# First up projection as seven half-size products per pair (Strassen's scheme), with the channel stage in six parts

## What is computed

```python
D_MODEL, SEQ, CTX_LEN = 1024, 512, 256
D_FF = ((8 * D_MODEL // 3 + 127) // 128) * 128      # 2816, 22 tiles of 128

def conv_ffn(h, w_up, conv_w, conv_b, w_down):
    u = h @ w_up                                    # tokens x 1024 by 1024 x 5632
    u = depthwise_conv_width_3(u, conv_w) + conv_b  # along the tokens
    g, v = jnp.split(u, 2, axis=-1)
    return (jax.nn.silu(g) * v) @ w_down

x_lat = x_lat + g2x * conv_ffn(modulate(rmsnorm(x_lat, g_ffn), sh2x, sc2x), ...)
x_ctx = x_ctx + g2c * conv_ffn(modulate(rmsnorm(x_ctx, g_ffn), sh2c, sc2c), ...)
```

## Time and profile before

| | |
|---|---|
| median of 3 runs | 1761.22 us (1761.12 to 1761.82) |
| profiled execution: time, span | 1760.48 us, 1758.7 us |
| mean granted TensorE clock | 0.979 |
| TensorE busy | 1658.7 us, 94% |
| VectorE, ScalarE, GpSimd busy | 1120.0, 769.9, 617.5 us |
| first layer's channel stage, about | 480 to 1034 us |

### The profile page before, as it was taken

One profiled execution on the slowest core, in us unless ns is written; L12 is line 12 of the kernel. 1 busy time (PEld: TensorE's weight loads), 2 busy tenths in 40 slices (PEclk: granted clock), 3 DMA queues, 4 the chain that ended last, 5 costly groups with the idle time before them and its releaser, 6 DMA issues.

```text
span 1758.7 us, 25943 instructions
## 1 busy us (share of the span) xinstructions
PE 1658.7 (94%) x9530; PEld 1403.9 (80%) x9530; DVE 1120.0 (64%) x1749; ACT 769.9 (44%) x1273; POOL 617.5 (35%) x311
## 2 busy tenths in 40 slices
PE   5999998889799999999999998999888999999997
PEld 3778786778688888888888886888666888888887
DVE  7986677677876575767245774677664864254256
ACT  6546676463253311332123344666554543243242
POOL 0356560210123243323422307564222154444442
PEclk9899999999899999999999999999999999999999
DMA  9520000024222333433434423000012133233232
GB/s 393 178 93 25 25 25 13 25 109 150 90 96 87 116 121 108 134 117 120 144 120 131 144 96 96 25 25 25 25 37 96 48 120 97 94 95 106 87 99 91
DMA packets 45533, 168.24 MB, mean 96 GB/s; under 512 B 4736, under 2 KB 6784, under 8 KB 43520
## 3 DMA queue, kind: packets, MB, share of 16 engines
q1 hardware_dynamic: 40896, 156.50, 26.4%
q10 hardware_dynamic: 4544, 10.49, 1.6%
HBM read 161.73 MB, written 5.24 MB: 95 GB/s over the span
## 4 chain that ended last, share of the span: by engine, by line
PE 73%; DVE 7%; issue 3%; ACT 2%; POOL 1%; DMA 1%; DVEq 0%; ACTq 0%; SPq 0%; POOLq 0%
PE ps L1254 22%; PE ps L1255 21%; PE ps L1256 21%; PE ps L1385 3%; PE ps L1399 2%; DVE junk_mid L2150 1%; PE ps L1418 1%; DVE sqsum L2220 1%; DVE nb L2408 1%; PE ps L1419 1%; DVE p_sb L2426 1%; POOL w_lo L1136 1%; ACT ptmp L1919 1%; DMA w_raw<-w_d 1%; DVE ht L2247 0%
## 5 line engine op out<-in xcount | busy, mean ns | idle before, releaser
L1136 POOL TENSOR_TENSOR w_lo<-w_raw,w_hi 128x1024 fp32r<-128x1024 f32 x175 | 444.3, 2541 | 933.2 <-ACT w_hi L1700 893.9
L1254 PE MATMUL ps<-h_hi,w_hi 128*128 128x512 f32 (+1 forms) x1592 | 570.3, 358 | 14.5 <-DVE h_lo L2255 6.8
L1255 PE MATMUL ps<-h_lo,w_hi 128*128 128x512 f32 (+1 forms) x1592 | 558.8, 351 | 0.0
L1256 PE MATMUL ps<-h_hi,w_lo 128*128 128x512 f32 (+1 forms) x1592 | 558.4, 351 | 0.0
L1254 PEld LDWEIGHTS ps<-h_hi,w_hi 128*128 128x128 f32 x1592 | 304.6, 191 | 63.4 <-issue 24.7
L1256 PEld LDWEIGHTS ps<-h_hi,w_lo 128*128 128x128 f32 x1592 | 304.2, 191 | 39.9
L1255 PEld LDWEIGHTS ps<-h_lo,w_hi 128*128 128x128 f32 x1592 | 305.1, 192 | 35.5
L1700 ACT ACTIVATE w_hi<-w_raw 128x1024 fp32r<-128x1024 f32 x188 | 198.3, 1056 | 240.8 <-PE ps L1256 222.5
L1254 PE MATMUL ps<-a_hi,w_hi 128*128 128x512 f32 (+1 forms) x552 | 191.8, 347 | 1.2 <-DVE a_lo L2622 1.2
L1255 PE MATMUL ps<-a_lo,w_hi 128*128 128x512 f32 (+1 forms) x552 | 191.5, 347 | 0.0
L1256 PE MATMUL ps<-a_hi,w_lo 128*128 128x512 f32 (+1 forms) x552 | 191.1, 346 | 0.0
(11 more groups left out here) (186 smaller groups left out, 2414.1 us busy)
## 6 DMA issues: line engine op xcount, KB each, us to landing
w_raw<-w_d SPq DMA_DIRECT2D x188, 512.0 KB, 3.5
ada_b<-ada_d SPq DMA_DIRECT2D x56, 512.0 KB, 4.2
ada_first<-first_d SPq DMA_DIRECT2D x8, 1024.0 KB, 20.4
ada_lead<-ada_d SPq DMA_DIRECT2D x14, 512.0 KB, 3.6
ada_mid<-ada_d SPq DMA_DIRECT2D x10, 512.0 KB, 5.1
x_sb<-x_d SPq DMA_DIRECT2D x2, 1536.0 KB, 9.0
x_sb<-x_d ACTq DMA_DIRECT2D x1, 3072.0 KB, 11.9
x_spill_d<-x_sb ACTq DMA_DIRECT2D x1, 2048.0 KB, 7.8
```

What stands on the lines that cost most here:

```text
L1136: nc.gpsimd.tensor_tensor(w_lo[:, c % RING, :], w_raw[:, c % RAW, :], w_hi[:, c % RING, :].bitcast(f32), ALU.subtract).then_inc(w_lo_done, 1)
L1254: nc.tensor.matmul(out, lh, rh, start=first, stop=False)
L1255: nc.tensor.matmul(out, lh, rl_, start=False, stop=False)
L1256: return nc.tensor.matmul(out, ll, rh, start=False, stop=last)
```

## The change

The first layer's stage has six parts, of 4, 4, 4, 4, 3 and 3 pairs. Part 0 keeps the ordinary units. In parts 1 to 5 (18 pairs) a pair is one 2 x 2 block product: the two halves of the features in (512 each, 4 blocks) by the two halves of the tokens (384 each), and the tiles g and v. The four quarters of its result come from seven products of half size instead of eight, each of 4 blocks x 3 matmuls of 384 columns:

- Sums of h (three forms `s_hi`, `s_lo` of 4 blocks, and a fourth that overwrites a quarter of `h_hi` and `h_lo`) are made once by VectorE, with copies to the high part by ScalarE: in part 0 behind each pair (`sums_of_h`) and at its first four down tiles (`s3_of_h`).
- Sums of weights are made for each pair by VectorE (`t_sums`, `t_last`, four of 128 x 512). Weights now come in halves of 128 x 512. There are four raw buffers of one half each, one for each role: of a pair, g's two halves are roles 0 and 3, v's are 1 and 2. A buffer is loaded again once the sums are made and the low part that reads it is done.
- Sums of products form in PSUM: ScalarE copies a half tile from one bank to another, and further products accumulate onto it (`seed`, twice a pair); ScalarE keeps one product in SBUF (`keep`), and VectorE adds it to two places (`join`, twice).
- VectorE makes two of the seven low parts of weights (`half_lo` of s1 t1 and s4 b22), GpSimd the other five. All weight work is done seven steps ahead (`made_ahead`), where a step is a half product or a down tile, with eight slots.
- Convolution, silu and the product of a pair are spread over the steps of the next pair. The last pair of a part is finished behind its last half product; down tiles 0 to 2 start with all pairs but the last.
- The adaLN columns are dealt anew: one behind each pair of part 0, one at down tiles 0 to 3 of part 0, one at each down tile of parts 1 to 4 (two at the first two of part 4) and at four of part 5, and one in each pair of parts 3 to 5. The first 64 of them have two streams.
- The loops over pairs become straight code. The rope tables give up their place to sums and are loaded again before layer 1.

The core of the diff (new functions and the new lists of VectorE and ScalarE):

```diff
-PARTS = [8, 8, FF_TILES - 16]
+PARTS = [[4, 4, 4, 4, 3, 3], [8, 8, FF_TILES - 16]]
...
+PRODUCTS = ["a11 b11", "a22 t4", "s2 t2", "s1 t1", "a12 b21", "s3 t3", "s4 b22"]
...
+def half_steps():
+    steps = [("down", 0, d) for d in range(KT)]
+    for part in range(1, len(PARTS[0])):
+        a11, a22, s2, s1, a12, s3, s4 = PRODUCTS
+        n = PARTS[0][part]
+        for g in range(n):
+            if g:
+                steps += [(p, part, g) for p in (a11,)] + [(a22, part, g - 1)]
+                steps += [(p, part, g) for p in (s2, s1, a12, s3, s4)]
+            else:
+                steps += [(p, part, g) for p in (a11, s1, s2, a12, s3, s4)]
+        steps.append((a22, part, n - 1))
+        steps += [("down", part, d) for d in range(KT)]
+    return steps
...
+LO_DVE = ("s1 t1", "s4 b22")
...
+        if kind == "down":
+            tiles = [int(n < KT - PARTS[0][0]), 1, 1, 1, 1 + (n < 2), int(n < 4)][part]
+        elif kind == "s2 t2":
+            tiles = int(part >= 3)
...
+        def wait_role_read(e, n):
...
+            if role in (0, 2):
+                e.wait_ge(t_sums_done, 4 * group_no(part, g) + 3)
+            wait_half_lo(e, STEP[("a11 b11", "s1 t1", "s4 b22", "a22 t4")[role], part, g])
...
+            def product(kind, part, g):
+                s = STEP[kind, part, g]
+                wait_half_lo(pe, s)
+                n, bank = group_no(part, g), pair_of(part, g)
+                down = down_unit(0, part - 1)
+                if kind == "a11 b11":
+                    if g >= 2:
+                        pe.wait_ge(taps_done, 2 * (n - 2) + 2)
+                    else:
+                        pe.wait_ge(bank_read, evac_index(down + KT - 4 + down_banks(part - 1).index(bank)) + 1)
+                        mark_written(side(bank, True), s)
+                elif kind == "s1 t1":
+                    if g:
+                        pe.wait_ge(kept, n)
+                    else:
+                        pe.wait_ge(bank_read, evac_index(down + KT - 2) + 1)
+                elif kind == "s2 t2":
+                    if g == 0:
+                        pe.wait_ge(bank_read, evac_index(down + KT - 3) + 1)
+                        mark_written(side(4, False), s)
+                    pe.wait_ge(seeded, 2 * n + 1)
+                elif kind == "s3 t3":
+                    pe.wait_ge(seeded, 2 * n + 2)
+                elif kind == "a22 t4":
+                    pe.wait_ge(joined, 2 * n + 1)
...
+                first = slice(0, KT // 2), slice(0, HALF)
+                out, f = {"a11 b11": (side(bank, False), (h_hi, h_lo, 0, 0)),
+                          "a12 b21": (side(bank, False), (h_hi, h_lo, KT // 2, 0)),
+                          "a22 t4": (side(bank, True), (h_hi, h_lo, KT // 2, HALF)),
+                          "s3 t3": (side(bank, True), (h_hi, h_lo, 0, HALF)),
+                          "s2 t2": (side(bank, True), (s_hi[1], s_lo[1], 0, 0)),
+                          "s1 t1": (ps[:, 6, 0:HALF], (s_hi[0], s_lo[0], 0, 0)),
+                          "s4 b22": (side(4, False), (s_hi[2], s_lo[2], 0, 0))}[kind]
+                fh, fl, k0, t0 = f
+                opens = kind in ("a11 b11", "s1 t1")
+                for k in range(KT // 2):
+                    mm = three(out, half_weights_of(s, k), (fh[:, k0 + k, t0:t0 + HALF], fl[:, k0 + k, t0:t0 + HALF]),
+                               opens and k == 0, k == KT // 2 - 1, not opens)
+                mm.then_inc(product_done, 1)
...
+            def t_sums(part, g):
+                n = 4 * group_no(part, g)
+                for role in range(3):
+                    dve.wait_ge(half_loaded[role], 16 * role_count(HALF_NO["b%d" % role, part, g]))
+                if n:
+                    old = (part, g - 1) if g else (part - 1, PARTS[0][part - 1] - 1)
+                    wait_half_lo(dve, STEP[("s3 t3",) + old])
+                    wait_half_lo(dve, STEP[("s2 t2",) + old])
+                    dve.wait_ge(t_sums_done, n)
+                else:
+                    dve.wait_ge(form_lo_done, 3 * KT // 2)
+                t_sum_at(t_sum[1][:, :], half_raw(2), half_raw(1))
+                dve.wait_ge(t_sums_done, n + 1)
+                t_sum_at(half_raw(1), half_raw(1), half_raw(0))
+                dve.wait_ge(t_sums_done, n + 2)
+                t_sum_at(t_sum[0][:, :], half_raw(2), half_raw(1))
+            def t_last(part, g):
+                n = 4 * group_no(part, g)
+                wait_half_lo(dve, STEP["a12 b21", part, g])
+                dve.wait_ge(t_sums_done, n + 3)
+                t_sum_at(half_raw(3), half_raw(3), t_sum[0][:, :])
...
+            def sums_of_h(k):
+                x, y, z = (t[:, :] for t in form)
+                if k:
+                    dve.wait_ge(form_lo_done, 3 * k)
+                whole(x, k, HALF)
+                whole(y, k + KT // 2, HALF)
+                whole(z, k, 0)
+                step.wait()
+                form_sum(y, x, y, ALU.add)
+                dve.wait_ge(forms_made, 3 * k + 1)
+                whole(x, k + KT // 2, 0)
+                form_sum(z, y, z, ALU.subtract)
+                step.wait()
+                dve.wait_ge(forms_made, 3 * k + 2)
+                form_sum(x, x, z, ALU.subtract)
...
+            def made_ahead(s):
+                if s + AHEAD >= len(STEPS):
+                    return
+                kind, part, n = STEPS[s + AHEAD]
+                if kind == "a11 b11":
+                    t_sums(part, n)
+                elif kind in LO_DVE:
+                    half_lo(s + AHEAD)
+                elif kind == "s3 t3":
+                    t_last(part, n)
...
+            def half_channel(update):
+                for s, (kind, part, n) in enumerate(STEPS):
+                    last = part == len(PARTS[0]) - 1
+                    if kind == "down":
+                        if part and n == 0:
+                            g = PARTS[0][part] - 1
+                            outer_taps(part, g, 0)
+                            gate_product(part, g)
+                            gate_lo(part, g)
+                        if part == 0:
+                            if n == 0:
+                                sums_of_h_lo(KT // 2 - 1)
+                                add_bias(5 * KT, 5 * KT + KT // 2)
+                            if n < KT // 2:
+                                s3_of_h(n)
+                            if n == KT // 2:
+                                add_bias(5 * KT + KT // 2, N_ADA)
+                        update(down_unit(0, part) + n, 5 * KT, n)
+                        if part == 0 and n < KT // 2:
+                            s3_of_h_lo(n)
+                        made_ahead(s)
+                        for c in ADA_AT[s]:
+                            ada_straight(c, c + 1, streams=2 if c < N_ADA + 2 * KT else 1)
...
+                    if kind == "a11 b11":
+                        if n:
+                            join(part, n - 1, True)
+                        made_ahead(s)
+                        if n:
+                            outer_taps(part, n - 1, 1)
+                    elif kind == "a22 t4":
+                        if n == PARTS[0][part] - 1:
+                            join(part, n, True)
+                            outer_taps(part, n, 1)
+                        made_ahead(s)
+                    elif kind == "s2 t2":
+                        if n:
+                            outer_taps(part, n - 1, 0)
+                        made_ahead(s)
+                        for c in ADA_AT[s]:
+                            ada_straight(c, c + 1, streams=1)
+                    elif kind == "a12 b21":
+                        if n:
+                            gate_product(part, n - 1)
+                        made_ahead(s)
+                    elif kind == "s3 t3":
+                        made_ahead(s)
+                        if n:
+                            gate_lo(part, n - 1)
+                    elif kind == "s4 b22":
+                        join(part, n, False)
+                        made_ahead(s)
...
+                    if kind == "a11 b11":
+                        if n:
+                            conv_start(part, n - 1, 1)
+                    elif kind == "a22 t4":
+                        if n < PARTS[0][part] - 1:
+                            seed(part, n + 1, 0)
+                        else:
+                            conv_start(part, n, 1)
+                    elif kind == "s2 t2":
+                        if n:
+                            conv_start(part, n - 1, 0)
+                        else:
+                            seed(part, n, 0)
+                    elif kind == "s1 t1" and n:
+                        seed(part, n, 1)
+                    elif kind == "a12 b21":
+                        if n == 0:
+                            seed(part, n, 1)
+                        keep(part, n)
+                        if n:
+                            gate_silu(part, n - 1)
+                    half_hi(s + AHEAD)
```

(2 more changed lines are left out.)

567 lines of the change are left out of this document (465 added, 102 removed).

## The result

The changed kernel takes **1867.49 us** (median of 4 runs, 1864.92 to 1871.52), the kernel before beside it 1761.17 (1760.23 to 1761.82): ratio 1.0607, 95% interval 1.0594 to 1.0619. The direction was forecast; the loss is twice the forecast one (+106 against +51), above the range.

The account below looks back on a forecast made before the run. TensorE, 94% busy, was taken to bound the kernel before, with VectorE making it wait after. Terms: -38.0 + 1.7 + 31 + 24 + 7 + 11 + 2.5 + 8 + 4 = +51 against 1760.48: 1812 us, range 1772 to 1840.

Parts of the forecast that it names:

- What is removed: Pairs of parts 1 to 5: 84 products of 384 columns at 0.1735 us; 18 pairs save 38.0 us (28 to 42).
- Part 0: VectorE's added sums of h delay part 0's down tiles and the first half product: loss 31 us (20 to 37).
- The long cycle: Later parts: VectorE's chain through b22's load makes a pair 17.8 us, 18.6 in parts 3 to 5; 24 lost together.
- Down steps with adaLN: Parts 1 and 2: s1 t1 waits for update 6's bank, 11 us together; part 4 loses 2.5.
- A collision: VectorE operations with two SBUF inputs and GpSimd's wait for each other's end; PSUM sums are free, else 2.4 us a pair.
- Ends of parts, and the turn: Last pair's tail outlasts covering down work: 7 us, 3.1 each in parts 4 and 5; turn to layer 1: 8.
- Clock: Waits of about 3.12 us in each part lower TensorE's clock, mostly while VectorE is late: 4 us (0 to 20).
- keep TensorE's pace: First rival: GpSimd's operations fall into gaps, b22 loads early, pair cycle 14.6 us; total 1769 us, chance 0.14.
- part 0's lateness: Second rival: four down-tile banks mostly absorb VectorE's lateness in part 0, which loses 8 us; total 1747 us, chance 0.08.
- The third: Rival: lower clock holds through the parts, 18 pairs lose 1.5 us each, 27 instead of 4; 1835 us, chance 0.10.
- my own case: Main case for the whole kernel: 1812 us, own range 1790 to 1838, chance 0.68.
- The signs: Layer 0's channel stage: VectorE over 80% busy, part 0 down-tile waits 20 us or more, later-pair seed waits, weight sums awaiting loads.

Follow-up runs that it names:

- the four products: Low-by-low product added in down tiles of part 0 and the last part, on the kernel with seeds and adaLN columns moved ahead: 1832.82 us.
- The two changes of order: On the changed kernel: seeds ahead of weight copies in ScalarE's list, 1846.3 us; adaLN columns ahead of halves in SyncE's queue, 1848.37; both together 1831.43.
- short lows: GpSimd's lows of half units cut to 64 columns: 1784.47 us on the kernel with both changes of order, 1828.13 on the changed kernel itself.
- The lows on VectorE: All seven lows of a pair made by VectorE, on the kernel with both changes of order (1831.4 us): 1834.79 us.

## Why the prediction was wrong in size

Forecast was a loss of 51 us, measured are 104 in the trace and 106 in the medians. A ledger of the stage, from the table: -38.0 saved, +2.6 marking products, part 0 +28.1 (2.6 of it ahead of its downs), pairs +89.1 over full pace (10.5, 22.8, 22.9, 11.8, 21.1), downs of part 4 +3.8, last part +18.1 (20.3 against 2.2 before); together +103.7, measured +103.8. Against the forecast, 38.0 of the missing 52.5 are one wait that the sum didn't have (the first pair's seed) and 20.3 the clock in the pairs (24.3 for 4); the ends and the turn add 6.9 and the marks 0.9, while the other waits of the pairs came out 10.7 below their terms and part 0 2.9.

- **What is removed:** right, with a price that was picked half way between two rows. Half products take 0.1735 us per step: 58.8 us for four pairs where nothing waits. The marks are fifteen, not ten (three a part): 2.6 for 1.7.
- **Part 0:** 31 forecast, 28.1 measured. TensorE's waits add up to 20.0 us only; its slower pace at a clock of 0.84 fills most of the rest (6.9 us within the downs), which the four products showed to cost nothing by itself.
- **The long cycle:** right. Forecast were 17.8 us and 18.6 with a column; measured are 17.6 to 18.3 in parts 1 and 2 and 18.3 to 19.3 in parts 3 to 5. VectorE's timeline has the same place of two successive pairs 17.60 us apart, and the wait behind the second sum that I put at 2.3 us (the profile has "issue" beside it; the load landed at 648.46), and then GpSimd beside the weight sum:

```profile
644.73 0.55 DVE L2753 TENSOR_TENSOR ps<-ps,shared 128x384 f32<-128x384 f32 x1
645.79 0.55 DVE L2745 TENSOR_TENSOR ps<-ps,shared 128x384 f32<-128x384 f32 x1
648.64 1.21 DVE L2663 TENSOR_TENSOR t_sum<-w_raw 128x512 f32<-128x512 f32 x1 [2.29 <-issue]
662.33 0.55 DVE L2753 TENSOR_TENSOR ps<-ps,shared 128x384 f32<-128x384 f32 x1
...
648.03 2.97 POOL L1369 TENSOR_TENSOR w_lo<-w_raw,w_hi 128x512 fp32r<-128x512 f32 x2 [4.64 <-ACT w_hi L2056]
```

  In the pairs TensorE is idle for 64.8 us: 38.0 for first seeds, 9.6 before s1 t1, 17.2 for all other waits, those of the cycle among them (24 forecast for the cycle). The other 24.3 of the 89.1 are a slower pace at the lower clock.
- **Down steps with adaLN: the step that failed.** It costed what the late update 6 does to s1 t1 (11, with 2.5 for part 4; 9.6 measured) and stopped there: "update 6 end at 37.4, with five GpSimd operations in the way at 43.2; s1 t1 needs that bank at 35.8". It didn't go on to what stands behind on VectorE (update 7, the second pair's weight sums), on ScalarE (a weight copy of such a sum, and behind it the seed) and on SyncE's queue (two columns behind four halves that VectorE's late low frees). The two changes of order showed both causes, 21 and 19 us. "s2 t2 can't start before" a seed was in the forecast for later pairs alone; the first pair I took for free.
- **A collision:** the mechanism was right. I gave it 1 to 2 us a cycle, 5 in a run of downs and 5 in part 0, and with that the cycle and part 0 came out; what shortening the lows would give I had far too low (16 for 47 us), with what else their length does (TensorE and the weight sums wait for them). The Trainium skill (SBUF — State Buffer, Who interferes with whom) says that "Issue order, not op shape, decides who blocks"; the trace agrees for one of the two orders: the same weight sum takes 0.68 us at 729.01, where GpSimd stands idle until 731.94, and 1.21 us at 648.64, begun 0.61 us behind GpSimd's subtraction. By that page the sums in PSUM stay free of it, and they do (0.55 us each). The words "fully blocks", quoted in the prediction, stand there for VectorE's two-port modes; of two inputs in SBUF the page says that they contend, and rows 7 and the weight sums above show how much.
- **Ends of parts, and the turn:** 3.8 for part 4 (3.1 forecast). For part 5 and the turn I had 3.1 + 8; it is 18.1. With four down tiles of 3.12 us a bank comes round before VectorE has updated it (a wait of 4.06 us before the last), and another 4.75 for the sum of squares.
- **Clock:** 4 forecast. Beside its waits TensorE was slower than at full pace by 6.9 us in part 0's downs, 24.3 in the pairs and some 5 in the last part. In part 0 that cost nothing, and in the last part keeping TensorE busy gave nothing back; in the pairs no run separates it from the waits: it vanished with them (mean clock 0.97 to 1.00 in the pairs of each part with short lows, 0.88 to 0.96 in the changed kernel).
- **The rivals:** none of the three as a whole. The pairs didn't keep TensorE's pace, and part 0's lateness wasn't absorbed. The third had one thing right that my own case had wrong: its 27 us for the clock in the pairs are near the 24.3 measured, where I took 4. Its 1835 is 32 us too low all the same: it hadn't the first pairs' seed waits either.
- **The signs:** VectorE was to be busy over 80%; it was 93% from 550 to 610 us and 74% from 610 to 1000. TensorE's idle time before down tiles 0 and 4 to 7 of part 0 was to be 20 us or more; it was 16.4, with 3.04 more before the first half product. The seed waits of second and third pairs came at 0.7 us each; the long ones stood in the first. The weight sums did wait for a load.
- **Slips in its working,** which change nothing: the terms of a pair in part 0 add up to 18.9 and not to about 18.5, the last ones of the long cycle to 16.9 and not to 16.7, and the product at 512.42 ends 0.83 us after GpSimd's pair of operations, not 0.96.

Open: how much of the 47 us is VectorE being kept waiting and how much the GpSimd low's own length on the way to a product. The lows on VectorE price only the first: about 0.61 us of VectorE for each low.

## What to carry to other kernels

A scheme that saves TensorE an eighth of its products pays only if the engines that make its sums have room. Here 38 us of products were traded for six operations a pair on VectorE and the sums of h, and VectorE with what it waits for then set the pace of part 0 and of the pairs; even with GpSimd's lows, the adaLN columns and the sums of h cut short and b22 loaded once a part, the weight sums staying whole, only 7 us were left. When one late item is found, follow every in-order list that it stands in, one by one, to the item that the bounding engine waits for: a seed behind a weight copy and columns behind halves in a queue were 36 of the 106 us, and undoing them took no work away. When several causes lie on one chain, what one of them gives when it is removed is not its share: take them out together as well. And price work "beside" on GpSimd as work on VectorE where both read two operands in SBUF, as it came out here.

## What the runs showed that I had not expected

GpSimd's subtraction of 512 columns takes 1.3 to 1.5 us, VectorE's 0.68, and moving 90 of them from the first to the second (76 in the window shown) changed the time by 3.4 us, within its spread. In part 0, where TensorE waits for VectorE, the lower clock cost nothing: 79 more products in 60 us at 0.94 instead of 0.86 left the end where it was.
